# Output stage of a token mixer: another order of branches, products by token tile, one addition on GpSimd

## The chip, the cores and the metric

One core of a Trainium2 chip runs the whole program, two transformer blocks over 256 tokens of width 1024. The metric is the device time of one execution in microseconds (us); lower is better. The changed stage is one of some twenty phases and is run once, at the end of the first block's token mixer.

## What is computed

```python
def token_mixer(h, w_in, qk_gain, ..., w_branch_a, w_branch_b, w_branch_c, w_out, rel_bias, i):
    ...                                  # three attentions: o_a, o_b, o_c
    o_b = rms_norm(o_b, diff_out_norm) * (1.0 - lam_init)   # over each head's 128 values
    g = sigmoid(gates.reshape(b, t, 3, D_MODEL))
    y = (g[:, :, 0] * (o_a @ w_branch_a) + g[:, :, 1] * (o_b @ w_branch_b)
         + g[:, :, 2] * (o_c @ w_branch_c))
    return y @ w_out                     # added to x
```

All is float32. `o_a` has 256 columns, `o_b` 512, `o_c` 256, and `w_out` is 1024 by 1024.

## The kernel before

Tokens stand on the 128 partitions as two token tiles (t = 0, 1). The 1024 columns of the attentions' output `o` are eight chunks of 128: 0 and 1 are branch a, 2 to 5 branch b, 6 and 7 branch c.

A float32 product is made of three products of rounded halves. An operand is split into a high half (ScalarE casts it, L173 for weights, L1149 for activations) and a low half (VectorE subtracts the high one from the whole, L180 and L1158). `product3` (L206 to 210) multiplies high by high, high by low and low by high. A product of 128x512 is one PE row of L208, L209 or L210. A weight tile is 256 rows of 1024 columns, 1 MB, for two chunks: for both token tiles it is used in 24 products of 128x512, so the eight tiles of this stage (one of a, two of b, one of c, four of `w_out`) make 192.

Weight tiles come in the order of one stream. `load_tiles` on the sync engine puts tile i into a ring of R = 4 slots when `tiles_split` shows that tile i - 4 is split. There are H = 3 pairs of split buffers: `split_hi` of tile s waits until `split_used` shows that the products of tile s - 3 are done. At the start of this stage the ring already holds its first four tiles. `wait_used` waits for `split_used` of a tile, and so for its last product.

The stage is `mixer_out`. Four engines run programs of their own, in the written order, and meet by semaphores. VectorE first finishes b's norm: squares from ScalarE, a reduction (L1207), a root on ScalarE (L1190), a reciprocal, and for each token tile a multiplication by the norm's weight `dnorm` (L1215) and by the reciprocal root (L1216). Only then TensorE turns `o` (L1134, sixteen transposes of 128x128 in four groups that share PSUM banks 0 and 1, so that the third group waits for the split of the first). Then the three branches follow one another, a, b, c, each for both token tiles in PSUM banks 4 to 7. Because they share these banks, TensorE waits with each branch until VectorE has multiplied the sums of the one before by the gates (L1229, L1232). VectorE also adds the branches (L1237). When y is complete for both token tiles, TensorE turns it in four groups through banks 0 and 1, their halves are split, and the product with `w_out` follows in banks 4 to 7. Two additions into x (L1249) end the stage. The sigmoid of all gates is one instruction for each token tile (3072 columns, L1196) on ScalarE.

At the end of each phase all engines meet before any starts the next. The next phase (`ffn_phase` with `Modulation`) uses GpSimd for products of the hidden values (L580) and for a decay table (L1598 to L1602).

Of the kernel before, what the change touches and what calls it, by code (L numbers as in the profile page):

```python
# [8 lines left out]
P = 128  # L9
# [1151 lines left out]
def mixer_out(nc, g, pr):  # L1161

    with ExitStack() as ctx:
# [9 lines left out]
        dnorm = sb("dnorm", [P, P])  # L1173
        br0 = g.stream.first["w_branch_a"]
        out0 = g.stream.first["w_out"]
        branch_tiles = [[0], [1, 2], [3]]
        tiles = list(range(br0, out0 + 4))
        block = ctx.enter_context(nc.Block(no_gpsimd_drain=True))

        @block.sync  # L1180
        def _(sp):
            sp.dma_start(dnorm[:], g.I["diff_out_norm"].to_broadcast([P, P])).then_inc(S["dnorm"], 16)
            load_tiles(g, sp, out0 + 4 + R)

        @block.scalar
        def _(act):
            for t in range(TT):
                nc.scalar.activation(sq[:, t], o[:, t, 256:768], ACT.Square).then_inc(S["sq"], 1)
            act.wait_ge(S["mean"], 1)
            nc.scalar.activation(st[:, :, 4:8], st[:, :, 0:4], ACT.Sqrt).then_inc(S["root"], 1)  # L1190
            for i in tiles[0:2]:
                split_hi(nc, g, act, i)
            turned_hi(nc, g, act, S, g.xt2, "ot", KC)
            for t in range(TT):
                gt = pr[:, t, GATE_COL:GATE_COL + 3 * D]
                nc.scalar.activation(gt, gt, ACT.Sigmoid).then_inc(S["gates"], 1)  # L1196
            for i in tiles[2:7]:
                split_hi(nc, g, act, i)
            turned_hi(nc, g, act, S, g.xt2, "yt", KC)
            split_hi(nc, g, act, tiles[7])  # L1200

        @block.vector
        def _(dve):
            ch = Chain(dve, S["dve"])
            v = nc.vector
            dve.wait_ge(S["sq"], TT)
# [5 lines left out]
            dve.wait_ge(S["dnorm"], 16)  # L1212
            for t in range(TT):
                o3 = o[:, t, 256:768].rearrange("p (h e) -> p h e", e=P)
                ch(v.tensor_tensor(o3, o3, dnorm[:].unsqueeze(1).to_broadcast([P, 4, P]), ALU.mult))  # L1215
                v.tensor_tensor(o3, o3, st[:, t, 0:4].unsqueeze(2).to_broadcast([P, 4, P]), ALU.mult).then_inc(S["b_normed"], 1)  # L1216
            for i in tiles[0:2]:
                split_lo(nc, g, dve, i)
            turned_lo(nc, g, dve, S, g.xt2, "ot", KC)
            for i in tiles[2:4]:  # L1220
                split_lo(nc, g, dve, i)
            dve.wait_ge(S["gates"], TT)
            for b in range(3):
                wait_used(g, dve, br0 + branch_tiles[b][-1])
                for t in range(TT):
                    gt = pr[:, t, GATE_COL + D * b:GATE_COL + D * b + D]
                    src = ps[:, 4 + 2 * t:6 + 2 * t, :].rearrange("p b n -> p (b n)")
                    if b == 0:
# [1866 lines left out]
```

## Time and profile before

| | us |
|---|---|
| median of 3 runs | 2575.21 |
| lowest, highest | 2564.55, 2588.22 |
| profiled execution, its time | 2587.78 |
| profiled execution, its span | 2585.9 |
| mean granted TensorE clock | 0.809 of full |

The span goes from the first to the last instruction of the profiled execution; 1.9 us of its time lie around it. All times of rows are microseconds from the start of the span. The granted clock (PEclk) is 1.00 at 2.4 GHz and 0.50 at 1.2 GHz. PEld is the loading of the stationary operand, which overlaps the products. A bracket at the end of a timeline row is the time for which the engine stood idle before it and what ended that. xN behind a row is the number of instructions merged in it.

### The profile page before, as it was taken

What the parts mean: (1) busy time and instruction counts of PE and PEld (TensorE: products, weight loads), DVE (VectorE), ACT (ScalarE), POOL (GpSimd) and SP (SyncE); (2) the same over time, 40 slices, a digit from 0 to 9 for tenths busy, and PEclk for the clock granted to TensorE, in tenths of its full rate; (3) what the DMA queues carried; (4) which work ended last, traced back from release to release, by engine and by line L of the source; (5) the groups of instructions that cost most, each with busy time, mean ns of one, the idle gap of its engine ahead of it and who ended that gap; (6) DMA issues with size and microseconds to landing.
All of it is one profiled execution on the core that took longest, in us unless ns stands there. A gap on an engine that the chain in (4) does not pass through costs nothing. (4 is left out here: it accounts for less than half of the span.)

```text
span 2585.9 us, 36557 instructions
## 1 busy us (share of the span) xinstructions
PE 1977.7 (76%) x15491; PEld 1284.4 (50%) x15491; DVE 895.7 (35%) x1285; ACT 582.9 (23%) x799; POOL 177.8 (7%) x269
## 2 busy tenths in 40 slices
PE   6999997857899967788687875866666666667665
PEld 5998995645788856687476864210110101111010
DVE  4654434563554566575556453100000000000000
ACT  3434443241433342133221331000000000000000
POOL 0100000000020023300334000000000000000000
PEclk9999998558899978879779786877767677776776
DMA  5655552002897430033000325899999999999997
GB/s 186 189 188 161 182 186 81 1 34 98 280 285 247 163 92 2 2 115 119 5 2 3 123 93 209 333 417 417 417 417 416 417 417 417 417 417 417 418 417 293
DMA packets 222640, 587.84 MB, mean 227 GB/s; under 512 B 11775, under 2 KB 144479, under 8 KB 189743
## 3 DMA queue, kind: packets, MB, share of 16 engines
q1 hardware_dynamic: 220662, 583.95, 59.9%
q8 instruction: 100, 1.64, 0.3%
q10 hardware_dynamic: 1848, 2.01, 0.2%
q14 instruction: 30, 0.24, 0.0%
HBM read 584.83 MB, written 1.09 MB: 227 GB/s over the span
## 5 line engine op out<-in xcount | busy, mean ns | idle before, releaser
L2873 PE MATMUL ps<-ex_ring,ex_xe 128*32 128x512 f32 x1536 | 284.5, 835 | 150.7 <-DMA ex_ring<-in_exp_w 150.7
L2948 DVE TENSOR_TENSOR ex_hid<-ps,ex_silu 128x512 f32<-128x512 f32 x16 | 11.1, 692 | 891.1 <-PE ps L2873 891.1
L2873 PEld LDWEIGHTS ps<-ex_ring,ex_xe 128*32 128x32 f32 x1536 | 36.7, 125 | 392.0 <-DMA ex_ring<-in_exp_w 371.1
L208 PE MATMUL ps<-xt_hi,ffn_whi 128*128 128x256 f32 x704 | 205.5, 292 | 6.8 <-DVE xt_lo L371 6.8
L2894 PE MATMUL ps<-ex_ring,ex_ht 128*32 128x512 f32 x768 | 147.6, 869 | 81.5 <-DMA ex_ring<-in_exp_w 75.8
L209 PE MATMUL ps<-xt_lo,ffn_whi 128*128 128x256 f32 x704 | 201.2, 286 | 0.0
L210 PE MATMUL ps<-xt_hi,ffn_wlo 128*128 128x256 f32 x704 | 201.0, 285 | 0.0
L180 DVE TENSOR_TENSOR ffn_wlo<-ring,ffn_whi 128x2048 fp32r<-128x2048 f32 x66 | 154.2, 2336 | 107.8 <-ACT ffn_whi L173 107.4
L173 ACT CAST ffn_whi<-ring 128x2048 fp32r<-128x2048 f32 x66 | 125.2, 1901 | 121.2 <-PE ps L210 102.8
L208 PEld LDWEIGHTS ps<-xt_hi,ffn_whi 128*128 128x128 f32 x704 | 136.8, 194 | 16.8 <-issue 16.6
L208 PE MATMUL ps<-mixin_whi,xt_hi 128*128 128x256 f32 (+1 forms) x496 | 139.8, 282 | 3.5 <-DVE xt_lo L371 3.5
L209 PE MATMUL ps<-mixin_wlo,xt_hi 128*128 128x256 f32 (+1 forms) x496 | 139.2, 281 | 0.0
L210 PE MATMUL ps<-mixin_whi,xt_lo 128*128 128x256 f32 (+1 forms) x496 | 139.2, 281 | 0.0
L209 PEld LDWEIGHTS ps<-xt_lo,ffn_whi 128*128 128x128 f32 x704 | 136.9, 194 | 1.2 <-issue 1.2
L210 PEld LDWEIGHTS ps<-xt_hi,ffn_wlo 128*128 128x128 f32 x704 | 136.7, 194 | 0.0
L2894 PEld LDWEIGHTS ps<-ex_ring,ex_ht 128*32 128x32 f32 x768 | 19.7, 129 | 196.6 <-DMA ex_ring<-in_exp_w 181.1
L2873 PE MATMUL ps<-ring,ex_xe 128*32 128x512 f32 x512 | 85.5, 765 | 41.2 <-DMA ring<-in_exp_w 41.2
L180 DVE TENSOR_TENSOR mixin_wlo<-ring,mixin_whi 128x2048 fp32r<-128x2048 f32 (+1 forms) x31 | 70.6, 2277 | 95.9 <-ACT mixin_whi L173 95.9
L208 PEld LDWEIGHTS ps<-mixin_whi,xt_hi 128*128 128x128 f32 x496 | 94.2, 190 | 3.9 <-issue 3.9
L210 PEld LDWEIGHTS ps<-mixin_whi,xt_lo 128*128 128x128 f32 x496 | 94.3, 190 | 0.0
L209 PEld LDWEIGHTS ps<-mixin_wlo,xt_hi 128*128 128x128 f32 x496 | 93.8, 189 | 0.0
L2914 ACT COPY ex_wselt<-ps 128x256 f32<-128x256 f32 x16 | 6.0, 372 | 304.7 <-PE ps L2879 304.7
(742 smaller groups left out, 3791.4 us busy)
## 6 DMA issues: line engine op xcount, KB each, us to landing
ex_ring<-in_exp_w SPq DMA_DIRECT2D x288, 1024.0 KB, 23.4
ring<-in_exp_w SPq DMA_DIRECT2D x96, 1024.0 KB, 24.3
ring<-in_w_in SPq DMA_DIRECT2D x55, 1024.0 KB, 5.2
ring<-in_ffn_w_gate SPq DMA_DIRECT2D x22, 1024.0 KB, 6.1
ring<-in_ffn_w_up SPq DMA_DIRECT2D x22, 1024.0 KB, 5.4
ring<-in_ffn_w_down SPq DMA_DIRECT2D x22, 1024.0 KB, 4.9
ffn_mod_tile<-in_mod_w SPq DMA_DIRECT2D x12, 1024.0 KB, 6.7
xn<-in_mod_w SPq DMA_DIRECT2D x12, 1024.0 KB, 6.8
```

What stands on the lines that cost most here:

```text
L173: nc.scalar.copy(g.whi[:, s % H, 0:n], g.ring[:, i % R, 0:n]).then_inc(g.hi_done, 1)
L180: nc.vector.tensor_tensor(g.wlo[:, s % H, 0:n], g.ring[:, i % R, 0:n], g.whi[:, s % H, 0:n].bitcast(F32), ALU.subtract).then_inc(g.tiles_s ...
L208: nc.tensor.matmul(out, lhs[0], rhs[0], start=start, stop=False, skip_group_check=shared)
L209: nc.tensor.matmul(out, lhs[0], rhs[1], start=False, stop=False, skip_group_check=shared)
L210: return nc.tensor.matmul(out, lhs[1], rhs[0], start=False, stop=stop, skip_group_check=shared)
L2873: mm = mm_(ps[32 * q:32 * q + 32, 4 + u, :], xe[:, k], expert_slot(g, n)[:, 512 * q:512 * q + 512], start=k == 0, stop=k == KC - 1)
L2894: mm = mm_(ps[32 * q:32 * q + 32, 7, :], ht[:, k % 4, CAP * f:CAP * f + CAP], w[:, h, 512 * n:512 * n + 512], start=k == 0, stop=k == KC - 1)
L2914: nc.scalar.copy(wselt[:], ps[:, 6, 0:T]).then_inc(S["wselt"], 1)
L2948: v.tensor_tensor(hid[:], ps[:, 5, :], silu[:], ALU.mult).then_inc(S["hid"], 1)
```

## The change

- The stream of weight tiles has the branches in the order a, c, b. In the new code `a, c, b0, b1` are the four tiles, `out0` the first of the output's.
- Chunks of a and c are turned first and split without waiting for b's norm; a's products follow. Then b's chunks are turned. The four groups have a PSUM bank each (0 to 3).
- The norm's weight is no multiplication of `o` any more: transposed, it is one value for each partition, and is the scale in the high and low split of b's chunks (`dnorm` is a column that is already on the chip, and its load goes).
- Each product of a weight tile is made for token tile 0 (12 products of 128x512), then for token tile 1, and VectorE can gate the first while the second runs (`first_summed`). c sums up in banks 0 to 3, a and b in banks 4 to 7.
- Gates are made by branch and token tile (1024 columns).
- GpSimd adds c's gated part to y; VectorE adds b's.
- y is turned by token tile, with a bank for each group. b1's product for token tile 1 stands between the turning of y for tile 0 and the first product with `w_out`.
- Splits, sigmoids and gatings are in the order written here on each engine.

In the diff "..." stands for removed and unchanged lines, which are in the listing above.

```diff
@@ -1160,6 +1160,8 @@
 def mixer_out(nc, g, pr):
...
@@ -1170,107 +1172,204 @@
...
+        dnorm = col(g, "diff_out_norm")
...
+        a, c, b0, b1 = range(br0, br0 + 4)
...
+        def turned_o(part, q):
+            x = g.xt2[part][:, :, P * (q % 2):P * (q % 2) + P]
+            x = x[:, 2:6] if q >= 2 else x.rearrange("p (m k) n -> p m k n", k=2)[:, 0:4:3]
+            return x, (ps[:, q, :].rearrange("p (k n) -> p k n", k=4) if q >= 2 else
+                       ps[:, q, :].rearrange("p (m k n) -> p m k n", m=2, k=2))
+        def turned_y(part, q):
+            return (g.xt2[part][:, 4 * (q % 2):4 * (q % 2) + 4, P * (q // 2):P * (q // 2) + P],
+                    ps[:, q, :].rearrange("p (k n) -> p k n", k=4))
+        def gate_of(branch, t):
+            return pr[:, t, GATE_COL + D * "abc".index(branch):GATE_COL + D * "abc".index(branch) + D]
+        def summed(bank, t):
+            return ps[:, bank + 2 * t:bank + 2 * t + 2, :].rearrange("p b n -> p (b n)")
         @block.sync
         def _(sp):
...
         @block.scalar
         def _(act):
+            def hi_o(q):
+                act.wait_ge(S["ot_turned"], q + 1)
+                dst, from_ = turned_o(0, q)
+                if q >= 2:
+                    nc.scalar.activation(dst, from_, ACT.Copy, scale=dnorm).then_inc(S["ot_hi"], 1)
+                else:
+                    nc.scalar.copy(dst, from_).then_inc(S["ot_hi"], 1)
+            def gates(branch):
+                for t in range(TT):
+                    gt = gate_of(branch, t)
+                    nc.scalar.activation(gt, gt, ACT.Sigmoid).then_inc(S["gates"], 1)
+            def hi_y(q):
+                act.wait_ge(S["yt_turned"], q + 1)
+                nc.scalar.copy(*turned_y(0, q)).then_inc(S["yt_hi"], 1)
+            split_hi(nc, g, act, a)
+            hi_o(0)
+            hi_o(1)
...
+            split_hi(nc, g, act, c)
+            gates("a")
+            hi_o(2)
+            hi_o(3)
+            split_hi(nc, g, act, b0)
+            gates("c")
+            split_hi(nc, g, act, b1)
+            gates("b")
+            split_hi(nc, g, act, out0)
+            hi_y(0)
+            hi_y(1)
+            split_hi(nc, g, act, out0 + 1)
+            hi_y(2)
+            hi_y(3)
+            split_hi(nc, g, act, out0 + 2)
+            split_hi(nc, g, act, out0 + 3)
+        @block.gpsimd
+        def _(pool):
+            for t in range(TT):
+                pool.wait_ge(S["gated"], 3 + t)
+                nc.gpsimd.tensor_tensor(y[:, t], y[:, t], tmp[:, t], ALU.add).then_inc(S["y_ac"], 1)
         @block.vector
         def _(dve):
...
+            def lo_o(q):
+                dve.wait_ge(S["ot_hi"], q + 1)
+                dst, from_ = turned_o(1, q)
+                hi = turned_o(0, q)[0].bitcast(F32)
+                if q >= 2:
+                    v.scalar_tensor_tensor(dst, from_, dnorm, hi, ALU.mult, ALU.subtract).then_inc(S["ot"], 1)
+                else:
+                    v.tensor_tensor(dst, from_, hi, ALU.subtract).then_inc(S["ot"], 1)
+            def gate(branch, t, dst, bank):
+                dve.wait_ge(S["gates"], 2 * "acb".index(branch) + t + 1)
+                if t:
+                    wait_used(g, dve, {"a": a, "c": c, "b": b1}[branch])
+                else:
+                    dve.wait_ge(S["first_summed"], "acb".index(branch) + 1)
+                return v.tensor_tensor(dst, summed(bank, t), gate_of(branch, t), ALU.mult)
+            def lo_y(q):
+                dve.wait_ge(S["yt_hi"], q + 1)
+                dst, from_ = turned_y(1, q)
+                v.tensor_tensor(dst, from_, turned_y(0, q)[0].bitcast(F32), ALU.subtract).then_inc(S["yt"], 1)
+            split_lo(nc, g, dve, a)
+            lo_o(0)
+            lo_o(1)
...
+            split_lo(nc, g, dve, c)
+            lo_o(2)
+            lo_o(3)
+            for t in range(TT):
+                gate("a", t, y[:, t], 4).then_inc(S["gated"], 1)
+            split_lo(nc, g, dve, b0)
+            for t in range(TT):
+                gate("c", t, tmp[:, t], 0).then_inc(S["gated"], 1)
+            split_lo(nc, g, dve, b1)
+            def add_b(t):
+                dve.wait_ge(S["y_ac"], t + 1)
+                ch(gate("b", t, tmp[:, t], 4))
+                v.tensor_tensor(y[:, t], y[:, t], tmp[:, t], ALU.add).then_inc(S["y"], 1)
+            add_b(0)
+            split_lo(nc, g, dve, out0)
+            lo_y(0)
+            lo_y(1)
+            add_b(1)
+            split_lo(nc, g, dve, out0 + 1)
+            lo_y(2)
+            lo_y(3)
+            split_lo(nc, g, dve, out0 + 2)
+            split_lo(nc, g, dve, out0 + 3)
+            for t in range(TT):
+                if t:
+                    wait_used(g, dve, out0 + 3)
+                else:
+                    dve.wait_ge(S["first_summed"], 4)
...
+                v.tensor_tensor(xs, summed(4, t), xs, ALU.add)
         @block.tensor
         def _(pe):
+            def turn(src, t, chunks, bank, turned):
+                for n, k in enumerate(chunks):
+                    mm = nc.tensor.transpose(ps[:, bank, P * n:P * n + P], src[:, t, P * k:P * k + P], g.ident[:])
+                mm.then_inc(S[turned], 1)
+            def part(i, t, k0, bank, first, last):
+                w = split_pair(g, pe, i, 2)
+                for n_chunk in range(2):
+                    for n in range(2):
+                        mm = product3(nc, ps[:, bank + 2 * t + n, :], [x[:, k0 + n_chunk, P * t:P * t + P] for x in g.xt2],
+                                      [x[:, n_chunk, 512 * n:512 * n + 512] for x in w], first and n_chunk == 0, last and n_chunk == 1)
+                return mm
+            for t in range(TT):
+                turn(o, t, (0, 1, 6, 7), t, "ot_turned")
+            pe.wait_ge(S["ot"], 2)
+            part(a, 0, 0, 4, True, True).then_inc(S["first_summed"], 1)
+            part(a, 1, 0, 4, True, True).then_inc(g.split_used, 1)
...
+            for t in range(TT):
+                turn(o, t, range(2, 6), 2 + t, "ot_turned")
+            part(c, 0, 6, 0, True, True).then_inc(S["first_summed"], 1)
...
+            part(c, 1, 6, 0, True, True).then_inc(g.split_used, 1)
+            pe.wait_ge(S["gated"], 1)
+            part(b0, 0, 2, 4, True, False)
+            part(b1, 0, 4, 4, False, True).then_inc(S["first_summed"], 1)
+            pe.wait_ge(S["gated"], 2)
+            part(b0, 1, 2, 4, True, False).then_inc(g.split_used, 1)
+            pe.wait_ge(S["y"], 1)
+            for half in range(2):
+                turn(y, 0, range(4 * half, 4 * half + 4), half, "yt_turned")
+            part(b1, 1, 4, 4, False, True).then_inc(g.split_used, 1)
+            pe.wait_ge(S["yt"], 1)
+            part(out0, 0, 0, 4, True, False)
+            pe.wait_ge(S["y"], 2)
+            for half in range(2):
+                turn(y, 1, range(4 * half, 4 * half + 4), 2 + half, "yt_turned")
+            part(out0 + 1, 0, 2, 4, False, False)
+            pe.wait_ge(S["yt"], 3)
+            part(out0, 1, 0, 4, True, False).then_inc(g.split_used, 1)
+            part(out0 + 1, 1, 2, 4, False, False).then_inc(g.split_used, 1)
...
+            part(out0 + 2, 0, 4, 4, False, False)
+            part(out0 + 3, 0, 6, 4, False, True).then_inc(S["first_summed"], 1)
+            part(out0 + 2, 1, 4, 4, False, False).then_inc(g.split_used, 1)
+            part(out0 + 3, 1, 6, 4, False, True).then_inc(g.split_used, 1)
 def token_product(nc, g, pe, lhs, i0, n_tiles, k0=0):
@@ -1313,7 +1412,7 @@
...
+    for b in "acb":
...
```

## Rows read from the trace of the kernel before

**Rows 1.** Windows: stretch, length, busy us per engine, PEclk, DMA share, GB/s.
```profile
450.00:556.00 106.00, 82.48 (x287) 62.16 (x286) 65.20 (x217) 32.01 (x91) 0.00 (x0) 0.50 0.00 1
556.00:650.00 94.00, 59.19 (x225) 46.66 (x226) 42.02 (x37) 28.94 (x24) 0.00 (x0) 0.77 0.27 90
```

**Rows 2.** Timeline of the stage's entry: start us, us, engine, line, operation [idle before].
```profile
556.48 1.15 ACT L1188 ACTIVATE proj<-o 128x512 f32<-128x512 f32 x2 [4.55 <-PEq L893]
557.65 1.28 ACT L1190 ACT_TABLE_LOAD   x1
557.66 1.22 DVE L1207 TENSOR_REDUCE st<-proj 128x8 f32<-128x1024 f32 x1 [1.54 <-ACT proj L1188]
...
562.46 4.48 DVE L180 TENSOR_TENSOR mixout_wlo<-ring,mixout_whi 128x2048 fp32r<-128x2048 f32 x2
...
562.60 1.97 PE L1134 MATMUL ps<-ident,o 128*128 128x128 f32 x8 [6.94 <-DVE o L1216]
...
570.97 0.79 PE L208 MATMUL ps<-mixout_whi,xt_hi 128*128 128x512 f32 x1 [1.40 <-DVE xt_lo L1158]
```

**Rows 3.** Timeline, PE restarts in the stage, its last addition, next phase's first transposes.
```profile
585.91 0.79 PE L208 MATMUL ps<-mixout_whi,xt_hi 128*128 128x512 f32 x1 [6.76 <-DVE proj L1229]
...
601.52 0.51 PE L208 MATMUL ps<-mixout_whi,xt_hi 128*128 128x512 f32 x1 [2.57 <-DVE proj L1232]
...
612.35 1.97 PE L1134 MATMUL ps<-ident,proj 128*128 128x128 f32 x8 [5.04 <-DVE proj L1237]
619.55 1.97 PE L1134 MATMUL ps<-ident,proj 128*128 128x128 f32 x8 [5.24 <-DVE xt_lo L1158]
...
647.22 2.35 DVE L1249 TENSOR_TENSOR x<-ps,x 128x1024 f32<-128x1024 f32 x2 [12.20 <-PE ps L210]
...
649.95 2.48 PE L343 MATMUL ps<-ident,x 128*128 128x128 f32 x16 [2.76 <-PEq L1163]
```

**Rows 4.** Waits of the weight queue (SP): total us, times, longest.
```profile
SPq L2738 <- PEq L2738: 27.9, 1, 27.9
```

**Rows 5.** Windows inside bursts of products, columns as in 1.
```profile
571.00:576.00 5.00, 5.00 (x12) 3.93 (x13) 0.00 (x0) 4.99 (x3) 0.00 (x0) 0.50 0.12 50
576.00:579.00 3.00, 3.00 (x14) 2.23 (x12) 0.25 (x1) 2.72 (x2) 0.00 (x0) 0.98 0.00 0
585.90:589.50 3.60, 3.59 (x9) 2.82 (x10) 0.00 (x0) 0.00 (x0) 0.00 (x0) 0.50 0.59 234
627.00:646.00 19.00, 19.00 (x84) 15.59 (x83) 2.29 (x1) 1.90 (x1) 0.00 (x0) 0.99 0.17 55
```

**Rows 6.** Grouped instructions, 553 to 662: shapes xcount, busy us, mean ns, idle before.
```profile
L180 DVE TENSOR_TENSOR mixout_wlo<-ring,mixout_whi 128x2048 fp32r<-128x2048 f32 x8 | 18.0, 2286 | 17.8 <-ACT mixout_whi L173 17.7
L173 ACT CAST mixout_whi<-ring 128x2048 fp32r<-128x2048 f32 x8 | 15.1, 1895 | 31.6 <-PE ps L210 31.6
...
L1196 ACT ACTIVATE proj<-proj 128x3072 f32<-128x3072 f32 x2 | 5.4, 2757 | 0.0
L1158 DVE TENSOR_TENSOR xt_lo<-ps,xt_hi 128x512 fp32r<-128x512 f32 x8 | 5.3, 685 | 2.8 <-ACT xt_hi L1149 2.8
L1232 DVE TENSOR_TENSOR proj<-ps,proj 128x1024 f32<-128x1024 f32 x4 | 4.9, 1224 | 16.6 <-PE ps L210 16.6
...
L1149 ACT CAST xt_hi<-ps 128x512 fp32r<-128x512 f32 x8 | 4.7, 586 | 15.4 <-PE ps L1134 15.4
...
L1215 DVE TENSOR_TENSOR o<-o,dnorm 128x512 f32<-128x512 f32 x2 | 1.4, 686 | 0.0
```

**Rows 7.** Timeline of GpSimd (POOL) in the next phase.
```profile
742.22 2.39 POOL L1598 TENSOR_TENSOR ffn_decay<-ffn_decay 128x1024 f32<-128x1024 f32 x1 [4.11 <-ACT ffn_decay L1584]
...
748.60 2.72 POOL L1601 TENSOR_TENSOR ffn_fsum<-ffn_fsum,ffn_fdiff 128x1024 f32<-128x1024 f32 x1
```

**Rows 8.** Timeline of VectorE in the same stretch.
```profile
744.12 0.69 DVE L611 TENSOR_TENSOR ffn_tmp<-ps,ffn_silu 128x512 f32<-128x512 f32 x1 [2.65 <-PE ps L210]
...
749.10 4.37 DVE L180 TENSOR_TENSOR ffn_wlo<-ring,ffn_whi 128x2048 fp32r<-128x2048 f32 x1
```

More of the change, by code:

```diff
@@ L1219, in _ @@
[L1219 to L1228, printed above, removed]
-                        ins = v.tensor_tensor(y[:, t], src, gt, ALU.mult)
-                        ch(ins) if t == 0 else ins.then_inc(S["gated"], 1)
-                    else:
-                        ins = v.tensor_tensor(tmp[:, t], src, gt, ALU.mult)
-                        ch(ins) if t == 0 else ins.then_inc(S["gated"], 1)
-                if b:
-                    dve.wait_ge(S["gated"], b + 1)
-                    for t in range(TT):
-                        ins = v.tensor_tensor(y[:, t], y[:, t], tmp[:, t], ALU.add)
-                        if b == 2:
-                            ins.then_inc(S["y"], 1)
-                        else:
-                            ch(ins)
@@ L1242, in _ @@
-            for i in tiles[4:7]:
-                split_lo(nc, g, dve, i)
-            turned_lo(nc, g, dve, S, g.xt2, "yt", KC)
-            split_lo(nc, g, dve, tiles[7])
-            wait_used(g, dve, out0 + 3)
-            for t in range(TT):
+            split_lo(nc, g, dve, c)
+            lo_o(2)
+            lo_o(3)
+            for t in range(TT):
+                gate("a", t, y[:, t], 4).then_inc(S["gated"], 1)
+            split_lo(nc, g, dve, b0)
+            for t in range(TT):
+                gate("c", t, tmp[:, t], 0).then_inc(S["gated"], 1)
@@ L1253, in _ @@
+            pe.wait_ge(S["ot"], 2)
+            part(a, 0, 0, 4, True, True).then_inc(S["first_summed"], 1)
+            part(a, 1, 0, 4, True, True).then_inc(g.split_used, 1)
             pe.wait_ge(S["b_normed"], TT)
-            turn_rows(nc, g, pe, S, o, "ot", KC)
+            for t in range(TT):
+                turn(o, t, range(2, 6), 2 + t, "ot_turned")
+            part(c, 0, 6, 0, True, True).then_inc(S["first_summed"], 1)
             pe.wait_ge(S["ot"], 4)
-            n_chunk = 0
-            for b, own in enumerate(branch_tiles):
-                if b:
-                    pe.wait_ge(S["gated"], b)
-                for i in own:
-                    w = split_pair(g, pe, br0 + i, 2)
-                    for c in range(2):
-                        first, last = i == own[0] and c == 0, i == own[-1] and c == 1
-                        for t in range(TT):
-                            for n in range(2):
-                                mm = product3(nc, ps[:, 4 + 2 * t + n, :], [x[:, n_chunk, P * t:P * t + P] for x in g.xt2],
-                                              [x[:, c, 512 * n:512 * n + 512] for x in w], first, last)
-                        n_chunk += 1
-                    mm.then_inc(g.split_used, 1)
```

22 lines of the change are left out of this document (removed).

## The prediction

> **What bounds the kernel now.** I read in this order: the windows view of the stretch, the timeline of the changed stage on each engine, the grouped instructions, then the queue that loads weights. The stage runs from 556.5 us, where the first of its instructions starts [rows 2], to 649.57 us, where the last two additions into x end (647.22 + 2.35) [rows 3]: 93.1 us. TensorE is busy 59.2 of 94 us and its granted clock is 0.77 on average [rows 1]. Look at the brackets of the PE rows: its stops are 6.9 us at the start and later 6.8, 2.6, 5.0 and 5.2 us [rows 2, 3]. Each is ended by VectorE, by DVE rows of this stage, and none by a load. So neither engine is full: the stage is a relay of TensorE, ScalarE and VectorE in which one stands while another works.
>
> What a microsecond here is worth: the stage is bracketed by points where all engines meet. The weight queue's wait at the head of the router phase is on PE (27.9 us) [rows 4]; that phase issues the first expert weights, so the load-bound tail cannot start before the earlier phases are done. I count a shorter stage in full.
>
> **Prices.** All 192 products of 128x512 stay. Where the granted clock reads 0.99 (2.4 GHz), 84 of them start in 19.00 us, 0.226 us each; where it reads 0.50 (1.2 GHz), 12 start in 5.00 us, 0.42 each [rows 5]. A group of 12 products (one weight tile for one token tile) is then 2.72 us at the upper level and 5.04 at the lower. Eight transposes take 1.97 us after a long stop and sixteen 2.48 us where the clock is up, so 1.24 for eight [rows 2, 3]. The split of a weight tile is 1.90 us on ScalarE and 2.29 on VectorE, a quarter of the activations 0.59 and 0.69, a gating or an addition of 128x1024 on VectorE 1.22 [rows 6]. The sigmoid costs 2.76 us for 3072 columns [rows 6], so 0.92 for 1024, with 1.28 for its table, the duration of the table load shown for the root [rows 2]. A GpSimd addition of 128x1024 took 2.39 us [rows 7].
>
> The clock: products began at 570.97 at half rate, and the granted clock was 0.50 until 576 and 0.98 after it, 4.9 us of work later; at 585.9 it took 3.6 us [rows 2, 5]. It was still up after stops of 2.57 and 2.76 us (the first product at 601.52 takes 0.51 us against 0.79 at 585.91), and down after 5.04 and 6.76 us [rows 3].
>
> **The change part by part, as one schedule.** All of its times are worked out from those prices.
>
> *Entry.* ScalarE splits a's tile 556.5 to 558.4, VectorE follows to 560.7. TensorE meanwhile turns a's and c's chunks (1.0 us for each token tile at half clock). Their high halves run 558.4 to 559.6 on ScalarE and the low ones 560.7 to 562.05 on VectorE. a's products begin at 562.05 instead of 570.97: 8.9 us earlier. It is possible because b's norm no longer stands ahead of them. The norm takes 4.80 us on VectorE from its reduction to the next split (562.46 - 557.66) [rows 2]; the multiplication by b's weight goes (2 x 0.69) [rows 6], since it is now a scale in b's splits, which I cost at nothing extra (upper end 0.7 us for each low half on VectorE). That leaves 3.4 us, 562.05 to 565.45, under a's products. The load of the weight goes too and was hidden.
>
> *a, then c.* 4.9 us at half rate hold 11.7 of a's 24 products, the other 12.3 take 2.8: a ends at 569.8. Eight transposes of b to 571.05, c's first half to 573.8, its second to 576.5. ScalarE: c's split 563.65 to 565.55, table and a's two sigmoids to 568.7, so neither is late. b's high halves end at 571.6, low halves at 572.35.
>
> *The tight place.* VectorE now has a row of work: a's two gatings to 574.8, split of b0 to 577.1, c's two gatings to 579.55, split of b1. TensorE waits for the splits: b0's first product starts at 577.1 (0.6 us idle) and ends its 12 at 579.8. GpSimd's first addition of c's part starts at 578.3 and lasts until 580.7, over the moment when VectorE wants b1's split. The trace shows the cost of that: the same split took 4.37 us from 749.10 while GpSimd's additions ran, where it normally takes 2.29; it ended 2.15 us after the GpSimd row of 748.60 + 2.72 had ended. An instruction with one input in PSUM went through in 0.69 us beside another GpSimd addition [rows 6 to 8]. So gatings run freely, and b1's split ends at 580.7 + 2.15 = 582.85. GpSimd's second addition then runs to about 585.3. TensorE stands for 579.8 to 582.85, 3.05 us.
>
> The rule of the Trainium skill here (SBUF — State Buffer, Who interferes with whom) is that a VectorE instruction with two SBUF inputs and a GpSimd instruction that reads SBUF share an interface, and that the one that issues first has it for its whole length. The row above agrees that one blocks. Both contenders here, b1's split and GpSimd's second addition, become ready within a tenth of a microsecond; if the rule gave GpSimd its two additions in a row, the split would end at 580.7 + 2.39 + 2.15 = 585.2. In the row, VectorE got in between two GpSimd instructions, and I take that.
>
> *b and the output.* b1's first half 582.85 to 585.6, b0's second half to 588.3 while VectorE gates and adds (585.6 to 588.0) — y of token tile 0 is ready in time. Four plus four transposes to 589.55, b1's second half to 592.3, out0's first to 595.0. VectorE: split of out0 to 590.3, y's low halves to 591.65, second gating and addition 592.3 to 594.75, split of out1 to 597.05. TensorE: transposes to 596.25, 0.8 us idle, then out1 and out0 to 605.2. out2's split ends at 601.0. out3's waits for out0's release at 602.5 and ends at 606.7. Four last groups of 12: 605.2 to 616.1; they are not waited for. One addition into x remains after the last product, 1.22, since the other lies under it: 617.35.
>
> *Sum.* 649.57 - 617.35 = 32.2 us. I take off 1 us for some twenty handovers at 0.05 us: **31 us**. A second way to count: 8.9 for the earlier start; the stops after the first product, today 6.8 + 2.6 + 5.0 + 5.2 and 1.4 before out0's first product (as long as the one at 570.97) [rows 2, 3], 21.0 together, become 0.6 + 3.05 + 0.8, so 16.5; 1.1 for the last addition; and one slow stretch of products instead of three (a, b and the output), two times some 4 us at 0.46 loss, 3.7. That is 30.2, and the 2 us to 32.2 are ends of bursts and rounding. Where the saved stops go is named above: the next late thing is VectorE, at 577 to 583 us.
>
> The profiled execution took 2587.8 us, so it would become 2556.8. The median of the runs shown is 2575.2, 12.6 below it, so I predict **2544 us**. Within 1% is about what measurement of this kernel cannot tell from no change; 31 us is 1.2%.
>
> **Bounds of what the trace does not show.** The rise of the clock at 3.6 instead of 4.9 us of work: 0.6 us better. The stop of 3.05 us lies between 2.76 (kept) and 5.04 (fell); nearer to the first, so kept; if it falls, 3.6 to 4.9 us of work at half rate cost 1.8 to 2.4. The order of the two contenders: 0 to 2.4 us, and then the stop would be 5.4 and the clock surely down, 4.8 together. b's scaled low halves: 0 to 1.4. A GpSimd addition of 2.72 instead of 2.39 us [rows 7]: 0.3. Worst together: 31 - 7 = 24; best 33.
>
> **Rivals.**
>
> 1. *GpSimd first.* The shared interface goes to GpSimd twice, or the stop of 3 us drops the clock. Price 2 to 7 us: 2549 with the middle of it. For it: the tie. Against: the row of 749.10. Chance 0.22.
>
> 2. *The clock never rises.* The attention stage ahead ran at 0.50 for all of 106 us though TensorE was busy 82.5 of them [rows 1]. If bursts of 2.72 us with stops between did the same here, all 192 products would cost 5.04 per 12: a to 572.1, transposes 574.1, c to 584.2, three halves of b to 599.3, then 1.97 + 10.1 + 1.97 to 613.3 and seven groups to 648.6, the addition to 649.8 and handovers to 650.8, later than 649.57: **2576 us, slower** than before by 1. It decides from about 160 products at the lower level (31 / 0.194). Against it: the new stops after 562 are 0.6, 3.05 and 0.8 us, and today's denser parts all reached 0.98. Chance 0.04.
>
> 3. *Given back later.* The stage ends early but a load or a queue of a later phase sets the end, and little or nothing is left: 2560 to 2575. For it: the chain at the end is made of loads. Against: those loads are issued behind the meeting points [rows 4], and this stage's four prefetched tiles of the next phase are released at 590 to 607, ahead of its end. Chance 0.08.
>
> 4. *The handing over costs less and the clock rises earlier*: 2541. Chance 0.06.
>
> The forecast has 0.60.
>
> **How the numbers follow.** The forecast's own range is 24 to 33 us of gain, 2542 to 2551, before the spread of runs. The three shown lie 11 below to 13 above their median, so a new median may be 8 to 12 off. That gives 2531 to 2564, which holds the forecast, rival 1 and part of rival 3. Faster by over 1% means under 2549.5: most of the forecast (0.50), two fifths of rival 1 (0.09), rival 4 (0.05): 0.64. Slower by over 1% needs rival 2 or 3 plus a bad spread: 0.03. The rest, 0.33, is within 1%.
>
> **What would show it.** In the changed profile: the first product 5.6 us after the stage's first instruction; the stage 61 to 63 us long; one half-clock stretch of products, at its beginning; b1's split longer than 2.29 us and a stop of some 3 us before b1; no stop over 1 us after the first turning of y; later phases of the same length. It would be wrong by a second half-clock stretch, by GpSimd's two additions back to back ahead of b1's split, by ScalarE late with b's high halves, or by a longer next phase.

## The result and the profile after

The changed kernel takes 2552.7 us (median of 20 runs, 2535.07 to 2571.15), the kernel before 2577.5 (20 runs, 2564.55 to 2592.11). The medians lie 24.8 us apart. The ratio is 0.9906, 95% interval 0.9885 to 0.9927: 24 us less, between 19 and 30. The profiled execution's span is 2562.6 us at a mean granted clock of 0.808.

The changed stage can be measured far more closely than the whole. I take it from ScalarE's first row behind the meeting point (556.48 before [rows 2], 553.87 after) to the next phase's first load, 649.90 before and this row after (timeline of the queue that issues loads):

```profile
616.74 0.34 SPq L1527 DMA_DIRECT2D ffn_mod_sel<-k_modsel  x1
```

That is 93.4 us before and 62.9 after, 30.5 less. The windows view of the stage, and of two stretches in it (columns as in [rows 1]):

```profile
553.80:616.80 63.00, 53.13 (x225) 42.12 (x225) 39.12 (x32) 28.59 (x27) 6.79 (x2) 0.90 0.40 134
579.60:583.40 3.80, 3.77 (x10) 2.95 (x11) 0.00 (x0) 0.00 (x0) 2.20 (x1) 0.55 0.71 236
583.40:586.70 3.30, 3.30 (x16) 2.61 (x14) 2.30 (x2) 0.00 (x0) 0.00 (x0) 1.00 0.11 46
```

TensorE, busy 59.2 of 94 us before [rows 1], is busy 53.1 of 63 now, at a granted clock of 0.90 instead of 0.77. Of the 30.5 us, 24.5 are idle time of TensorE that is gone (34.3 us before, 9.8 now), and 6.0 are busy time (59.1 and 53.1), since the same products and transposes run at a higher granted clock. The clock is below 1.00 at the entry, up to 562.9, and once more, as the second row shows: for 3.8 us right behind the stop before b1. The third row has it at 1.00 again. First TensorE's timeline from the start to b0's first product:

```profile
553.84 1.94 PE L1327 MATMUL ps<-ident,o 128*128 128x128 f32 x8 [0.85 <-PEq L893]
559.35 0.79 PE L208 MATMUL ps<-mixout_whi,xt_hi 128*128 128x512 f32 x1 [3.56 <-DVE xt_lo L1263]
...
566.57 1.03 PE L1327 MATMUL ps<-ident,o 128*128 128x128 f32 x8
...
573.95 0.47 PE L208 MATMUL ps<-mixout_whi,xt_hi 128*128 128x512 f32 x1 [0.83 <-DVE mixout_wlo L180]
```

The turning of `o` (L1327) starts with the stage and no longer waits 6.9 us for the norm. a's first product is at 559.35, 5.5 us behind the stage's first row, where it was 14.5 [rows 2]. The second turning (566.57) and c's products have no stop before them; b0's first product (573.95) waited 0.83 us for the split. Then the next stops:

```profile
576.54 0.40 PE L210 MATMUL ps<-mixout_whi,xt_lo 128*128 128x512 f32 x1
579.63 0.58 PE L208 MATMUL ps<-mixout_whi,xt_hi 128*128 128x512 f32 x1 [2.69 <-DVE mixout_wlo L180]
...
580.43 0.63 PE L210 MATMUL ps<-mixout_whi,xt_lo 128*128 128x512 f32 x1
...
586.91 1.09 PE L1327 MATMUL ps<-ident,proj 128*128 128x128 f32 x8
...
593.44 1.09 PE L1327 MATMUL ps<-ident,proj 128*128 128x128 f32 x8
595.64 0.50 PE L208 MATMUL ps<-mixout_whi,xt_hi 128*128 128x512 f32 x1 [1.11 <-DVE mixout_wlo L180]
```

Where [rows 3] have stops of 6.76, 2.57, 5.04 and 5.24 us, the largest left is 2.69, before b1's first product (579.63); the two turnings of y (586.91 and 593.44) have no stop before them. The durations around 579.63 show the clock: 0.40 us for the product ahead of the stop, 0.58 for the first behind it, 0.63 for those that follow, which is the lower level. VectorE and GpSimd (POOL) in the same stage:

```profile
555.80 2.29 DVE L180 TENSOR_TENSOR mixout_wlo<-ring,mixout_whi 128x2048 fp32r<-128x2048 f32 x1 [2.35 <-ACT mixout_whi L173]
558.01 1.28 DVE L1263 TENSOR_TENSOR xt_lo<-ps,xt_hi 128x512 fp32r<-128x512 f32 x2
...
567.93 1.41 DVE L1261 SCALAR_TENSOR_TENSOR xt_lo<-ps,va,xt_hi 128x512 fp32r<-128x512 f32 x2 [2.95 <-ACT xt_hi L1208]
...
575.99 3.59 DVE L180 TENSOR_TENSOR mixout_wlo<-ring,mixout_whi 128x2048 fp32r<-128x2048 f32 x1
584.37 1.23 DVE L1271 TENSOR_TENSOR proj<-ps,proj 128x1024 f32<-128x1024 f32 x1 [4.79 <-PE ps L210]
585.63 1.22 DVE L1303 TENSOR_TENSOR proj<-proj 128x1024 f32<-128x1024 f32 x1
...
609.69 1.22 DVE L1321 TENSOR_TENSOR x<-ps,x 128x1024 f32<-128x1024 f32 x1 [3.96 <-PE ps L210]
615.18 1.22 DVE L1321 TENSOR_TENSOR x<-ps,x 128x1024 f32<-128x1024 f32 x1 [4.27 <-PE ps L210]
```

```profile
575.01 6.79 POOL L1249 TENSOR_TENSOR proj<-proj 128x1024 f32<-128x1024 f32 x2 [418.47 <-DVE proj L1271]
```

b1's split (575.99) takes 3.59 us where the other splits take 2.29. It ends at 579.58, and b1's first product starts at 579.63. GpSimd's two additions merge to 6.79 us from 575.01: by the 2.42 us that one takes alone (e8, below) the first runs to about 577.4, VectorE's split goes in between, and the second follows it. The additions into x (L1321) no longer stand together at the end: one is at 609.69, under products, one at 615.18.

### The profile page after: what moved, and what is told of

It reads as the page before. It is cut to its first block and busy times, and to the rows that moved or that the text cites. A ratio compares the mean times of both kernels' runs of the same rounds, so it can differ in the third digit from the quotient of the medians.

```text
span 2562.6 us, 36565 instructions
## 1 busy us (share of the span) xinstructions
PE 1982.8 (77%) x15491; PEld 1291.8 (50%) x15491; DVE 893.4 (35%) x1281; ACT 581.9 (23%) x803; POOL 184.3 (7%) x271
## 3 DMA queue, kind: packets, MB, share of 16 engines
HBM read 584.77 MB, written 1.09 MB: 229 GB/s over the span
## 6 DMA issues: line engine op xcount, KB each, us to landing
ring<-in_exp_w SPq DMA_DIRECT2D x96, 1024.0 KB, 24.8
```

## The experiments

The stage is 30.5 us shorter, the whole 24 (19 to 30). So two questions are open: what in the stage made the 30.5, and whether the later phases give something back. (The context and hyena phases are later phases of the program; the stretch between them is taken from the first load of the one, `head_sum`, to the first of the other, `hy_fz`.) **Theory A**: the stage's gain counts in full, and the rest is scatter of the later phases with TensorE's granted clock. **Theory B**: the later phases are longer behind the changed stage. **Theory C**: they depend on when they start. For each profiled execution the table has the stage, the stretch from the context phase to the hyena phase, and all after the stage, up to the store of the result; then the times of the runs. A ratio compares 20 runs (the changed kernel), 6 (e3, e8, e10) or 12 (e11, e12) with 20, 11, 11 and 23 runs of the kernel before that were taken beside them.

| kernel | stage us | context to hyena | all after the stage | run(s), median us | ratio to before (95%) |
|---|---|---|---|---|---|
| before | 93.4 | 297.6 | 1929.2 | 2577.5 | |
| changed | 62.9 | 310.8 | 1939.1 | 2552.7 | 0.9906 (0.9885 to 0.9927) |
| e1 before again | 93.7 | 291.9 | 1915.5 | 2572.2, one | |
| e2 changed again | 63.0 | 293.4 | 1921.9 | 2549.7, one | |
| e3 b1's split first | 59.5 | 307.8 | 1935.9 | 2555.5 | 0.9924 (0.9896 to 0.9951) |
| e4 norm first | 66.3 | 295.8 | 1919.1 | 2550.1, one | |
| e5 additions on VectorE | 63.8 | 295.3 | 1921.6 | 2548.7, one | |
| e6 weight multiplied | 62.7 | 292.0 | 1918.9 | 2545.5, one | |
| e7 both token tiles | 69.0 | 295.8 | 1916.3 | 2550.0, one | |
| e8 buffer of its own | 58.4 | 304.8 | 1926.8 | 2545.3 | 0.9881 (0.9850 to 0.9913) |
| e9 before, third | 93.7 | 290.4 | 1922.7 | 2578.2, one | |
| e10 changed, third | 62.9 | 292.2 | 1918.2 | 2543.4 | 0.9867 (0.9826 to 0.9908) |
| e11 pad of 30 us | 93.2 | 291.7 | 1919.1 | 2581.8 | 1.0012 (0.9983 to 1.0040) |
| e12 pad of 15 us | 78.0 | 289.7 | 1910.5 | 2556.6 | 0.9923 (0.9893 to 0.9952) |

**e1 and e2, the two kernels again** (no edit).

> The kernel before once more, for its phases. Both profiled executions taken so far differ by 30.5 us in the changed stage (93.4 and 62.9 us from its first row to the next phase's) but by only 23.3 us in the whole, since the stretch from the context phase to the hyena phase took 297.6 us before and 310.8 us after. Theory A (the later phases scatter from execution to execution with TensorE's granted clock, whatever the stage did): stage 93.4 +- 1 us, that stretch anywhere from 295 to 312. Theory B (the later phases are longer because of the change): stretch within 2 us of 297.6.

> The changed kernel once more, for its phases. Theory A: stage 62.9 +- 2 us (the clock's rise and whether it falls in the stop before b1), stretch from context to hyena phase anywhere from 295 to 312 us. Theory B: stretch at 310 +- 3 us again.

The stages came back within 0.3 us: 93.7 and 63.0. The stretch took 291.9 and 293.4 us; neither 297.6 nor 310.8 is a property of its kernel. It is the same code with the same number of products in each. Theory B's 310 for the changed kernel is out; a difference of a few us between the means isn't, with this scatter.

**e3, b1's split ahead of c's gatings.**

```diff
-            for t in range(TT):
-                gate("c", t, tmp[:, t], 0).then_inc(S["gated"], 1)
             split_lo(nc, g, dve, b1)
+            for t in range(TT):
+                gate("c", t, tmp[:, t], 0).then_inc(S["gated"], 1)
```

> VectorE splits b1's tile before it gates c's sums, so that GpSimd's addition cannot stand in its way. In the changed kernel this split took 3.59 us beside GpSimd, TensorE stood 2.7 us before b1 and its clock fell (9 of the next products at the lower level, 1.8 us). Theory of the prediction (the interface shared with GpSimd and the order on VectorE make the stop): the split takes 2.29, the stop goes, the clock stays up, and the stage is 4 to 5 us shorter than 62.9, so about 58; the whole about 2548 against 2577 of the kernel before, ratio 0.9885. Rival (VectorE is full there, and the work only moves): y of token tile 0 is later by two gatings and by GpSimd's addition, and the stage stays at 61 to 64.

VectorE's, GpSimd's and TensorE's timelines of e3:

```profile
575.18 2.29 DVE L180 TENSOR_TENSOR mixout_wlo<-ring,mixout_whi 128x2048 fp32r<-128x2048 f32 x1 [0.19 <-ACT mixout_whi L173]
577.38 2.35 DVE L1271 TENSOR_TENSOR proj<-ps,proj 128x1024 f32<-128x1024 f32 x2
581.12 1.23 DVE L1271 TENSOR_TENSOR proj<-ps,proj 128x1024 f32<-128x1024 f32 x1 [1.38 <-POOL proj L1249]
582.38 2.15 DVE L1303 TENSOR_TENSOR proj<-proj 128x1024 f32<-128x1024 f32 x1
```

```profile
578.68 4.77 POOL L1249 TENSOR_TENSOR proj<-proj 128x1024 f32<-128x1024 f32 x2 [421.76 <-DVE proj L1271]
```

```profile
584.59 1.09 PE L1327 MATMUL ps<-ident,proj 128*128 128x128 f32 x8 [0.82 <-DVE proj L1303]
```

The split takes 2.29 us and TensorE doesn't stop before b1, nor does its clock fall: the stage is 59.5 us, 3.4 less than 62.9, a little short of the 4 to 5 us expected and well below the rival's 61 to 64. The rest went into two new waits, both on GpSimd: VectorE waits 1.38 us for GpSimd's first addition before it gates b (581.12), and its own addition takes 2.15 instead of 1.22 us (582.38), while GpSimd's second addition runs until 578.68 + 4.77 = 583.45. TensorE then stands 0.82 us for y (584.59). The whole doesn't show the 3.4 us. It is 20 us under the kernel before (13 to 27), where the stage is 34 us shorter: by this interval a part of the stage's gain is missing from the whole. Its profiled execution has 307.8 us in the scattering stretch.

**e4, the norm first again.** The squares, root and scaling are ahead of a's split on both engines, and

```diff
+            pe.wait_ge(S["b_normed"], TT)
             for t in range(TT):
                 turn(o, t, (0, 1, 6, 7), t, "ot_turned")
```

> The changed kernel with b's norm ahead of everything again: squares, root and scaling first, then a's split and the first transposes, which wait for the norm. All else as changed. If the early start is worth what the prediction says, a's first product is 5 to 7 us later (the norm without the multiplication by its weight, 4.8 - 1.4 + 1.15 for the squares) and the stage 66 to 69 us instead of 62.9, partly made up since b's chunks then are ready sooner. Rival (VectorE's row from b's low halves to b1's split sets the stage, not the start): under 2 us.

TensorE in e4, whose stage starts at 556.11:

```profile
560.78 1.97 PE L1327 MATMUL ps<-ident,o 128*128 128x128 f32 x8 [5.50 <-DVE o L1286]
564.32 0.80 PE L208 MATMUL ps<-mixout_whi,xt_hi 128*128 128x512 f32 x1 [1.57 <-DVE xt_lo L1263]
```

a's first product is 8.2 us behind the stage's start instead of 5.5, and the stage 66.3 us, 3.3 longer. I had expected the product 5 to 7 us later; it is 2.7 later, since a's split on ScalarE now overlaps the norm's work on VectorE. Of the 9.0 us by which the change starts a earlier, then, the norm's place is worth about 3. The other 6 are what the kernel before did ahead of its first product besides: the multiplication by the norm's weight (2 x 0.69 us [rows 6]), a second tile's split (4.48 us for the two) and four turned groups through two banks, with a stop of 1.4 us before the first product [rows 2] and one of 3.03 before the third group:

```profile
567.61 1.97 PE L1134 MATMUL ps<-ident,o 128*128 128x128 f32 x8 [3.03 <-DVE xt_lo L1158]
```

These 6 us are read from the rows; no run undid them one by one.

**e5, c's part added on VectorE.**

```diff
-        @block.gpsimd
-        def _(pool):
-            for t in range(TT):
-                pool.wait_ge(S["gated"], 3 + t)
-                nc.gpsimd.tensor_tensor(y[:, t], y[:, t], tmp[:, t], ALU.add).then_inc(S["y_ac"], 1)
...
+            for t in range(TT):
+                dve.wait_ge(S["gated"], 3 + t)
+                v.tensor_tensor(y[:, t], y[:, t], tmp[:, t], ALU.add).then_inc(S["y_ac"], 1)
             split_lo(nc, g, dve, b1)
```

> The changed kernel with c's part added to y by VectorE, both additions ahead of b1's split; GpSimd does nothing in the stage. The split falls back from 3.59 to 2.29 us, but two additions (2.45 us) stand ahead of it: it ends 1.2 us later. Theory of the prediction (GpSimd's additions are worth little where they are, since they hold up the split as long as one addition takes): stage 64 +- 1 us against 62.9 and 63.0, the stop before b1 3.8 instead of 2.7. Rival (the additions on GpSimd are worth their 2.45 us in full): 65.5 or more.

VectorE and TensorE in e5:

```profile
576.99 2.35 DVE L1294 TENSOR_TENSOR proj<-proj 128x1024 f32<-128x1024 f32 x2
579.26 2.28 DVE L180 TENSOR_TENSOR mixout_wlo<-ring,mixout_whi 128x2048 fp32r<-128x2048 f32 x1
```

```profile
581.59 0.79 PE L208 MATMUL ps<-mixout_whi,xt_hi 128*128 128x512 f32 x1 [3.64 <-DVE mixout_wlo L180]
```

Two additions take 2.35 us, the split 2.28, and b1 starts behind a stop of 3.64 us. The stage is 63.8: moving the additions to GpSimd is worth 0.9 us here, not 2.35, since GpSimd blocks the split for 1.3 of them.

**e6, the norm's weight multiplied into `o` again.** Plain copies in b's splits, the weight loaded as before, and

```diff
                 o3 = o[:, t, 256:768].rearrange("p (h e) -> p h e", e=P)
...
+                ch(v.tensor_tensor(o3, o3, dnorm[:].unsqueeze(1).to_broadcast([P, 4, P]), ALU.mult))
```

> The changed kernel with the weight of b's norm multiplied into o again (two VectorE instructions of 0.69 us and the load of the weight), plain copies in b's splits. In the changed kernel VectorE waits 3.0 us for b's high halves right behind c's split, and TensorE is still at a's products when the norm ends, so the multiplication should be hidden: stage 63.0 +- 0.3 us. Rival (it is part of the gain): 64.4.

VectorE in e6:

```profile
565.37 2.28 DVE L180 TENSOR_TENSOR mixout_wlo<-ring,mixout_whi 128x2048 fp32r<-128x2048 f32 x1
569.27 1.29 DVE L1258 TENSOR_TENSOR xt_lo<-ps,xt_hi 128x512 fp32r<-128x512 f32 x2 [1.62 <-ACT xt_hi L1208]
```

The split of c starts 1.3 us later in the stage than in the changed kernel, and the wait for b's high halves behind it shrinks from 2.95 to 1.62 us. The stage is 62.7: the weight in the splits bought nothing.

**e7, no order by token tile.** Waits for whole tiles on VectorE, the sums of both token tiles gated and added together, and on TensorE

```diff
-            pe.wait_ge(S["gated"], 1)
+            pe.wait_ge(S["gated"], 2)
             part(b0, 0, 2, 4, True, False)
-            part(b1, 0, 4, 4, False, True).then_inc(S["first_summed"], 1)
-            pe.wait_ge(S["gated"], 2)
             part(b0, 1, 2, 4, True, False).then_inc(g.split_used, 1)
...
+            part(b1, 0, 4, 4, False, True)
             part(b1, 1, 4, 4, False, True).then_inc(g.split_used, 1)
...
             pe.wait_ge(S["yt"], 4)
...
+            for m in range(4):
+                part(out0 + m, 0, 2 * m, 4, m == 0, m == 3)
+                part(out0 + m, 1, 2 * m, 4, m == 0, m == 3).then_inc(g.split_used, 1)
```

> The changed kernel without the order by token tile: sums are gated when both token tiles are done, b0 is used for both before b1, y is added and turned for both, then the output's product begins, and its sums are added to x after all products. Gain: b0's second half covers b1's split, so no stop there (2.7 us and the fall of the clock). Loss: TensorE stands while VectorE gates and adds y (2.5 us), again until all of y is split (about 4 us, the clock falls), and one more addition ends the stage (1.2). Theory of the prediction: stage 67 to 69 us instead of 62.9. Rival (the order by token tile gives nothing, the early start gives all): 62 to 64.

TensorE in e7 around the turning of y:

```profile
590.49 1.09 PE L1317 MATMUL ps<-ident,proj 128*128 128x128 f32 x8 [2.67 <-DVE proj L1298]
592.88 1.97 PE L1317 MATMUL ps<-ident,proj 128*128 128x128 f32 x8 [1.30 <-DVE proj L1298]
597.47 0.79 PE L208 MATMUL ps<-mixout_whi,xt_hi 128*128 128x512 f32 x1 [2.63 <-DVE xt_lo L1271]
```

Stops of 2.67, 1.30 and 2.63 us stand there, the second group of transposes takes 1.97 us and the first product of the output 0.79, both at the lower level. The stage is 69.0 us, 6.1 longer, although the stop before b1 is gone. The order by token tile is the largest single part that was undone. The four parts undone alone (norm 3.3 us, GpSimd 0.9, weight 0, order by token tile 6.1) make 10.3 of the 30.5 us. The other 20 are not split up by a run: that they come from the PSUM banks (four for the turned groups, and c's sums apart from a's and b's), from the second tile's split behind a's products and from b standing last is read from which stops are gone.

**e8, b's gated part in a buffer of its own, GpSimd's second addition later** (on top of e3).

```diff
-                dve.wait_ge(S["y_ac"], t + 1)
-                ch(gate("b", t, tmp[:, t], 4))
-                v.tensor_tensor(y[:, t], y[:, t], tmp[:, t], ALU.add).then_inc(S["y"], 1)
+                ch(gate("b", t, own[:, t], 4))
+                dve.wait_ge(S["y_ac"], t + 1)
+                v.tensor_tensor(y[:, t], y[:, t], own[:, t], ALU.add).then_inc(S["y"], 1)
...
                 pool.wait_ge(S["gated"], 3 + t)
+                if t:
+                    pool.wait_ge(g.tiles_split, out0 + 1)
```

> As with b1's split first (stage 59.5 us), and two edits: b's gated part goes to a buffer of its own, so that its gating doesn't wait for GpSimd's addition of c's part, and GpSimd's second addition waits for out0's split. In the run before, VectorE waited 1.4 us for GpSimd, its own addition took 2.15 us beside GpSimd's second one, and TensorE stood 0.82 us for y. If the shared interface is all of it: that addition 1.22 us, y 1.4 us earlier, the stop of 0.82 gone, stage 58.5 to 58.8 us, the whole 34.8 us under the kernel before less what the later phases scatter: 2538 to 2552. Rival (GpSimd's second addition now stands in the way of y's second tile): stage 59.5 to 61.

VectorE and GpSimd in e8:

```profile
582.23 1.23 DVE L1274 TENSOR_TENSOR proj<-ps,proj 128x1024 f32<-128x1024 f32 x1 [1.25 <-PE ps L210]
583.49 1.23 DVE L1306 TENSOR_TENSOR proj<-proj 128x1024 f32<-128x1024 f32 x1
```

```profile
579.93 2.42 POOL L1252 TENSOR_TENSOR proj<-proj 128x1024 f32<-128x1024 f32 x1 [422.22 <-DVE proj L1274]
587.07 2.42 POOL L1252 TENSOR_TENSOR proj<-proj 128x1024 f32<-128x1024 f32 x1 [4.72 <-DVE mixout_wlo L180]
```

The addition takes 1.23 us, GpSimd's two stand apart at 2.42 each, and neither VectorE nor TensorE waits for them. The two edits were made together, so the 1.1 us that they win over e3 are not divided between them. The stage is 58.4 us, 4.5 under the changed kernel's, and the whole 2545.3 us, ratio 0.9881 (0.9850 to 0.9913). It is the shortest stage of all; in the whole it is 31 us under the kernel before (22 to 39), which doesn't separate it from the changed kernel.

**e9 to e12, the later phases.** The two kernels once more, and the changed kernel with a pad that nothing needs, ahead of the last addition into x (12 additions in e12):

```diff
+                if t:
+                    for _ in range(24):
+                        ch(v.tensor_tensor(tmp[:, 0], y[:, 0], y[:, 1], ALU.add))
                 xs = g.x[:, t]
```

> A third look at the kernel before, for its later phases (next phase to the end, the sum of all stretches behind the stage). So far 1929.5 and 1915.5 us in two executions of it, and 1939.0, 1921.3 (changed), 1935.9, 1919.3, 1921.9, 1919.3, 1916.4 and 1926.6 us in the eight with a shorter stage. Theory A (scatter only): 1915 to 1940. Theory B (later phases are some 5 us longer behind the shorter stage, as the 24.8 us of the whole against 30.5 in the stage suggest): 1915 to 1922.

> The changed kernel, timed beside the two with a pad on the same chip. Theory A: 30.5 us under the kernel before, within the interval of about 6. Theory B: 25 us under it.

> The changed kernel with 24 dependent VectorE additions of 128x1024 ahead of the last addition into x: about 30 us of work that nothing needs, on the path of the stage. The next phase then starts when it does in the kernel before. If each microsecond of the stage counts (theory A), the whole is 30 +- 1 us over the changed kernel plus up to 2 us for the next phase's first transposes at the lower clock, and so as long as the kernel before within 2 us. If the later phases are longer by what the changed stage leaves behind rather than by when they start (theory B), it is 5 us over the kernel before; if by when they start (theory C), 25 us over the changed kernel and as long as the kernel before.

> Half the pad, 15 us. Theory A: 15 +- 1 us over the changed kernel plus up to 2. Theory C (the later phases depend on when they start): anything from 5 to 25 over it, since where they start relative to what sets the clock is new.

The pad in e11's VectorE timeline:

```profile
616.21 30.17 DVE L1322 TENSOR_TENSOR proj<-proj 128x1024 f32<-128x1024 f32 x24 [4.27 <-PE ps L210]
```

With it the stage is 93.2 us and the whole 2581.8, ratio 1.0012 to the kernel before: a stage of the old length gives the old time. With half of it the stage is 78.0 us and the whole 21 us below the kernel before, where 15.5 were taken off. The changed kernel beside them is 34 us below (24 to 45). These four fit theory A. They don't exclude theory B, whose 5 us over the kernel before lie inside e11's interval (4 below to 10 above), nor do they decide on theory C: all after the stage took 1919.1, 1910.5 and 1918.2 us for three different starts of the next phase (648, 632 and 617 us), one execution each, where executions of one kernel differ by up to 21 us. The three executions of the kernel before average 1922.5 us after the stage and the three of the changed one 1926.4, or 1919.1 and 1920.1 without the first of each (e1 and e9, e2 and e10).

All runs together lean to a small loss. The interval of the first comparison (19 to 30 us) just leaves out 30.5, and e3's leaves out 34. A least-squares estimate from all 42 runs of the kernels with a shorter stage and no pad, each against the runs of the kernel before beside it, has the whole 4.9 us longer than the stage's shortening says, with a 95% interval of 1.6 to 8.3 (3.3 us, -0.2 to 6.8, without e3); the 24 runs with a pad have 0.7 (-4 to 5). The stretch from context to hyena points the same way: it took over 304 us in three of the nine executions with a shorter stage and no pad, and 298 or less in the other six and in all five of the kernel before and the padded ones. So theory A is not shown in full: most of the 30.5 us reach the end, some 5 may not, and no run tells why.

What scatters goes with the clock. The windows view of the stretch, context to hyena phase, in four executions, the kernel before and e9 first:

```profile
908.00:1205.60 297.60, 236.82 (x3200) 216.31 (x3200) 193.56 (x304) 87.92 (x134) 57.91 (x93) 0.83 0.22 67
```

```profile
905.10:1195.50 290.40, 228.56 (x3200) 208.55 (x3200) 193.61 (x305) 87.72 (x135) 57.84 (x93) 0.86 0.22 69
```

then the changed kernel and e10:

```profile
874.50:1185.40 310.90, 252.00 (x3200) 231.20 (x3200) 193.69 (x304) 87.61 (x134) 57.78 (x93) 0.79 0.21 64
```

```profile
874.10:1166.30 292.20, 232.93 (x3200) 211.55 (x3200) 193.83 (x304) 87.86 (x134) 58.73 (x93) 0.85 0.22 69
```

VectorE's and ScalarE's busy times are the same to 0.3 us and TensorE has 3200 instructions in each. Its busy time goes from 228.6 to 252.0 us as the mean granted clock goes from 0.86 to 0.79, and the stretch from 290.4 to 310.9.

## Why the prediction was right, and where it was off

The forecast was 31 us less, from a range of 24 to 33 for the stage; the stage gave 30.5. The time, 2552.7, lies in the stated range, 8.7 us above the stated value: 6.2 since the medians are 24.8 us apart, 2.3 since the kernel before has 2577.5 us over 20 runs where the forecast started from 2575.2.

- **What bounds the stage** was read rightly. The stops were handovers between engines, and taking them away took the time away. After its first transposes TensorE now stands 8.2 us in all: 3.6 before a, 0.8, 2.7 and 1.1.
- **Entry.** Forecast: first product 5.6 us after the stage's start; measured 5.5. The forecast took b's norm to be what makes it possible. e4 shows that the norm's place makes 3 of the 9 us; the rows put the rest on the shorter chain ahead of a.
- **The weight in the splits costs and gives nothing**: forecast so, and e6 shows it (62.7 against 62.9 and 63.0).
- **GpSimd and the split.** Forecast: b1's split blocked until GpSimd's first addition ends, then 2.15 us more, ending 26.35 us into the stage. Measured: 3.59 us for the split, ending at 25.7. VectorE was served between the two additions, as the forecast had read from the row of 749.10 [rows 8], in all eight executions with this order (3.57 to 3.61 us for the split). The rule of the Trainium skill (SBUF — State Buffer, Who interferes with whom) that such a pair blocks for a whole instruction agrees with this: the split ends 2.15 us behind GpSimd's first addition (about 577.4), and in e3 VectorE's addition takes 2.15 us instead of 1.22. That GpSimd might keep the interface for both was not seen.
- **The stop of 3 us and the clock** is the step that failed. The forecast kept the clock up behind a stop of 3.05 us, as nearer to one of 2.76 us that it called kept; the clock fell behind a stop of only 2.69 us. b1's first twelve products took from 579.63 to the gating at 584.37, 4.7 us instead of 2.7, so 2.0 us were lost. That was priced as a bound (1.8 to 2.4) and is half of the first rival. The premise was a misreading: behind the stop of 2.76 us [rows 3] the clock was still up when the transposes began and fell while they ran, as the windows of the kernel before show (columns as in [rows 1]):

```profile
650.40:650.80 0.40, 0.40 (x6) 0.40 (x5) 0.00 (x0) 0.40 (x1) 0.00 (x0) 1.00 0.00 0
651.20:651.80 0.60, 0.60 (x6) 0.60 (x5) 0.00 (x0) 0.60 (x2) 0.23 (x2) 0.50 0.32 66
```

  So the 2.48 us of these sixteen transposes are no price for a clock that is up, either; in the changed kernel eight take 1.03 to 1.09 us, not 1.24. At the entry the clock rose after 3.5 us of work instead of 4.9 (559.35 to 562.9), which gave back 0.6.
- **The sum of the stage** came out closer than its terms. The forecast's schedule is 60.85 us long without its 1 us for handovers; to the end of the last addition the changed stage took 62.5. It was 0.6 us ahead of the schedule at b1's first product (25.8 instead of 26.35) and 2.3 us longer from there on, 2.0 of it by the clock. The early rise and the allowance for handovers made up for the fall: in that the 30.5 beside 31 is luck.
- **The order by token tile** was forecast to leave no stop over 1 us behind the first turning of y. There is one of 1.1, before out1. e7 prices this part at 6.1 us.
- **The sum against the whole.** 30.5 us in the profiled stage became 24 (19 to 30) between runs. "I count a shorter stage in full" is the term that was mis-sized, by about 5 us (1.6 to 8.3) over all runs; the cause stays open. The pad alone fits counting in full. The later phases scatter by 29 us between executions (1910.5 to 1939.1 us), so the forecast should have given the microseconds after the stage a spread of their own, beside that of the runs.
- **The rivals.** GpSimd first: its clock half came true, its order of the two contenders did not. The clock that never rises: not here, 0.90 over the stage. Given back later: hardly anything being left, as that rival had it, is out; some 5 us may be, as above.

## What to carry to other kernels

In a relay of engines, count who waits for whom at each handover before looking at busy shares: here 30 us came from the order of work and separate banks, with the 192 products unchanged. An addition moved to GpSimd is worth its full time only if no VectorE instruction with two SBUF inputs is due meanwhile (0.9 us of 2.35 here); put one with a PSUM input there, or let GpSimd wait, as e8 does. A mean over a row can hide a change of clock inside it: look at short stretches of it before calling a clock kept. Compare one stage by its own rows between the meeting points: they repeat to 0.3 us where the whole scatters by 1%.

## What the runs showed of the hardware

The granted clock can fall after TensorE has started again, and the length of the last stop alone doesn't tell whether it will. It stayed at 1.00 for the next 5.7 us of products behind a stop of 2.57 us in the kernel before [rows 3], and so behind 2.58 us in e1 and e9. It fell behind the one of 2.69 us in the changed kernel, where the first product behind the stop still took 0.58 us and the next ones 0.63 (0.55 on average for 3.8 us), and likewise behind stops of 2.66 to 2.69 us in e2, e4, e6, e10, e11 and e12. Behind 2.76 us in the kernel before it fell after about 1.2 us of transposes. Behind 2.77 us in e7 it stayed up for all sixteen of the same transposes, which took 1.94 us instead of 2.48:

```profile
625.05 1.94 PE L343 MATMUL ps<-ident,x 128*128 128x128 f32 x16 [2.77 <-PEq L1165]
```

In the stretch from the context to the hyena phase the same instructions ran at a mean granted clock between 0.79 and 0.86. TensorE's busy time there moved by 23 us and the stretch by 20 from one execution to another, while VectorE's and ScalarE's busy times stayed, in both kernels.
